# A fused retention and latent-attention trunk: the last four modulation vectors moved from the retention stage to the latent stage, and rows turned to columns by DMA

## The chip, the cores and the metric

The kernel runs on one core of a Trainium2 chip. Its time is device microseconds (us) of one execution. The engines are TensorE (PE in the profile, PEld its weight loads), VectorE (DVE), ScalarE (ACT), GpSimd (POOL) and SyncE (SP), which here does little but issue DMAs.

## The reference, cut to what matters

Everything is float32, with 256 tokens of width 1024 and two layers. Layer 0 mixes by retention, layer 1 by latent attention (MLA) over a key and value side made from the stream after layer 0. Both have a mixture of 16 experts, two chosen for each token.

```python
c_act = silu(c)                                   # one row of 1024
for layer in range(2):
    mod = c_act @ w_mod[layer] + b_mod[layer]     # 1024 x 6144
    sh1, sc1, g1, sh2, sc2, g2 = split(mod, 6)
    if layer == 0:
        xn = rms_norm(h, norm_mix[0]) * (1 + sc1) + sh1
        mix = retention_mixer(xn, ...)            # w_in 1024 x 6144, w_out 2048 x 1024
    else:
        sh_kv, sc_kv = split(c_act @ w_mod_kv + b_mod_kv, 2)
        hn = rms_norm(h, norm_kv) * (1 + sc_kv) + sh_kv
        k_nope, k_rope, v = mla_shared_kv(hn, ...)
        xn = rms_norm(h, norm_mix[1]) * (1 + sc1) + sh1
        mix = mla_attention(xn, ..., k_nope, k_rope, v)
    h = h + g1 * mix
    xn = rms_norm(h, norm_ffn[layer]) * (1 + sc2) + sh2
    h = h + g2 * grouped_moe(xn, ...)             # 16 experts of 3 x 2.1 MB
return rms_norm(h, final_norm)
```

So there are 14 modulation vectors: six of each layer and two for the key and value side. Four of them are gates (g1, g2 of both layers), the others are shifts and scales. Layer 1's g1 is first used when the attention's output product is done, and its sh2, sc2 and g2 in its experts.

## The kernel before, in words

**Streaming.** Nearly all bytes are weights, each read once. SP loads them in a fixed order into a ring of six slots of 2.1 MB (L139). Item i waits until item i-6 is used up (`released`, L406 to L414); every item is loaded as two halves. SP works strictly in order, so an item whose slot is not free holds back all behind it. `STREAM` (L101 to L117) is the order for the retention stage: blocks of the input matrix (`win`), halves of modulation vectors (`mod`) and blocks of the output matrix (`wout`). A vector's 4.2 MB are two `mod` items m = 2v and 2v+1 of vector v in `MODV` (L78): v = 2 and 5 are layer 0's gates, 10 and 13 layer 1's gates; 11 and 12 are layer 1's sh2 and sc2.

**A vector.** DVE multiplies an item into a tile `part` with four instructions of 128x1024 (`mod_main`, L1463), each waiting for the one before. PE then sums over the partitions: for a gate with a matrix of ones, two products of 128x512 into bank 5, each added to the gate's bias by DVE (`gate_sum` L594, `gate_store` L1486; bank 5 is one buffer, so the second product waits for the first store); for a shift or scale with a one-hot block, into one row of bank 4 (L611 to L616). All eight rows stay in that bank. After the last, ACT copies the bank to SBUF and PE turns the rows to columns with 24 small products, once in the order that modulates activations (L766) and once in the order that the router wants (L769). DVE adds the biases and makes the scales (L1569 to L1584) and folds layer 0's scale into the router's weights (`router_prep`, L1586).

**Retention.** Twelve rounds, one for each `win` block, of 13.7 us of matmuls and small work (L675 to L730). `MODS_PER_ROUND` (L103) says which modulation items a round handles: one in round 2, three in round 3 and two in each after it. The four that remain (`LAST_MODS`, 24 to 27) are handled among the eight blocks of the output product (`wout`, L745 to L773).

**Experts.** For each of 8 pairs of experts, a round of 25.9 us on PE per 64 tokens of the busier expert: gather, gate, up and down products. Layer 0 has 8 rounds, layer 1 has 9 (one pair needs two). The next pair's gate, up and down matrices (12.6 MB) are loaded as this pair's are used up (`reload`, L458). Ahead of the first pair SP issues its two gate and two up matrices, waits for the attention's (or the retention's) last heads, issues its down matrices into space outside the ring (L441 to L450), then the second pair's gate matrices (L451).

**Latent stage.** Its six items (L125) take the six slots as layer 0's last experts free them. PE makes the latents (L999, L1007, L1015), DVE and ACT normalise them, PE turns and expands them (L1022 to L1063), then come eight heads and the output product (L1122). `router_prep(1)` stands ahead of the latents on DVE (L1752), and `fixed_logits(1)` behind L999 on PE.

## Time and profile before

| what | value |
|---|---|
| time, median of 3 runs | 935.76 us (935.08 to 938.44) |
| the profiled execution's own time | 935.13 us |
| its span, first to last instruction | 933.4 us |
| PE busy | 860.8 us, 92% |
| DVE, ACT, POOL busy | 323.8, 171.1, 156.8 us |
| DMA | 317.12 MB, mean 340 GB/s |
| chain that ended last | PE 72%, DMA 17%, DVE 5% |

The profile follows one execution. Its part 2 cuts the span into 40 slices of 23.3 us and shows how busy each engine was, the TensorE clock that was granted, and what the DMA moved. The chain is followed back from the last instruction, at each step to what released it. Times of rows count from the span's start.

### The profile page before, as it was taken

How to read it: one execution, taken by the hardware profiler on the slowest of the kernel's cores; microseconds unless marked ns; L12 is line 12 of the kernel's file. 1: busy time of each engine (PE TensorE's matmuls, PEld its weight loads, DVE VectorE, ACT ScalarE, POOL GpSimd, SP SyncE). 2: the span in 40 equal slices, each digit the busy share in tenths (PEclk: the TensorE clock that was granted, in tenths of full speed). 3: DMA queues.
4: the chain of work that ended last, by engine and by line, in shares of the span. 5: the costliest groups of instructions: out<-in, count | busy, mean ns of one | idle time of the engine just before them, and what ended most of it. 6: DMA issues, size and time to landing. Idle time of an engine off the chain costs nothing.

```text
span 933.4 us, 12095 instructions
## 1 busy us (share of the span) xinstructions
PE 860.8 (92%) x4387; PEld 479.3 (51%) x4388; DVE 323.8 (35%) x592; ACT 171.1 (18%) x339; POOL 156.8 (17%) x272
## 2 busy tenths in 40 slices
PE   6996899999999799999899879899899999999985
PEld 3785344444445554555354428684455554555442
DVE  2748568669723411111111123350411111111103
ACT  2100011121100312221201111251322212211111
POOL 0022100000001721222200121400632221111011
PEclk9998899999999899999989898999899999999988
DMA  9999999899847989999999995525469999399995
GB/s 324 387 357 372 369 377 381 326 378 379 317 180 323 403 328 421 415 422 422 423 422 421 388 358 213 206 90 202 159 249 424 416 396 422 137 390 423 422 379 170
DMA packets 68645, 317.12 MB, mean 340 GB/s; under 512 B 8935, under 2 KB 9066, under 8 KB 43262
## 3 DMA queue, kind: packets, MB, share of 16 engines
q1 hardware_dynamic: 61274, 304.42, 81.6%
q0 software_dynamic: 4976, 8.40, 3.6%
q10 hardware_dynamic: 2356, 3.76, 1.2%
q8 instruction: 26, 0.43, 0.2%
q14 instruction: 13, 0.11, 0.0%
HBM read 311.31 MB, written 15.20 MB: 350 GB/s over the span
## 4 chain that ended last, share of the span: by engine, by line
PE 72%; DMA 17%; DVE 5%; issue 2%; ACT 1%; SPq 1%; POOL 0%; ACTq 0%; DVEq 0%; POOLq 0%
PE bank L701 12%; PE bank L887 12%; DMA ring<-in_moe_w_up 8%; PE bank L905 8%; PE bank L874 8%; PE bank L739 6%; DMA h<-outs 6%; PE bank L849 5%; PE bank L642 3%; PE bank L1122 3%; DMA outs<-arena,row_id 2%; DVE part L1478 2%; PE bank L1077 1%; PE bank L897 1%; DMA ring<-in_w_mod 1%
## 5 line engine op out<-in xcount | busy, mean ns | idle before, releaser
L887 PE MATMUL bank<-ring,arena 128*64 128x256 f32 x1088 | 132.6, 399 | 18.7 <-DMA ring<-in_moe_w_up 18.7
L887 PEld LDWEIGHTS bank<-ring,arena 128*64 128x64 f32 x1088 | 83.8, 144 | 68.1 <-issue 39.1
L1722 DVE TENSOR_TENSOR arena<-bank,arena 128x256 f32<-128x256 f32 x34 | 20.9, 616 | 277.0 <-PE bank L887 277.0
L1478 DVE SCALAR_TENSOR_TENSOR part<-ring,cpad,part 128x1024 f32<-128x1024 f32 x84 | 109.0, 1297 | 21.2 <-DMA ring<-in_w_mod 16.4
L701 PE MATMUL bank<-ring,xnT 128*128 128x512 f32 x256 | 112.1, 596 | 0.0
L905 PE MATMUL bank<-ring,arena 128*64 128x512 f32 x480 | 109.3, 596 | 2.5 <-issue 2.5
L874 PE MATMUL bank<-ring,arena 128*64 128x512 f32 x480 | 106.3, 595 | 0.0
L701 PEld LDWEIGHTS bank<-ring,xnT 128*128 128x128 f32 x256 | 48.6, 192 | 61.7 <-issue 61.7
L849 PEld LDWEIGHTS bank<-arena,y 128*128 128x128 f32 x544 | 66.7, 204 | 17.5 <-issue 17.5
L849 PE MATMUL bank<-arena,y 128*128 128x128 f32 x544 | 69.8, 290 | 3.4 <-issue 3.4
L874 PEld LDWEIGHTS bank<-ring,arena 128*64 128x64 f32 x480 | 33.1, 137 | 60.2 <-issue 60.0
L905 PEld LDWEIGHTS bank<-ring,arena 128*64 128x64 f32 x480 | 33.3, 137 | 58.9 <-issue 56.7
L1274 ACT ACTIVATE arena<-bank,modc,scale 128x128 f32<-128x128 f32 x68 | 25.6, 456 | 184.4 <-PE bank L849 184.4
L1876 POOL DMA_INDIRECT outs<-arena,row_id x17 | 17.9, 1056 | 216.1 <-DVE arena L1732 135.6
L1732 DVE SCALAR_TENSOR_TENSOR arena<-bank,info,gate 128x512 f32<-128x512 f32 x34 | 25.5, 751 | 73.2 <-PE bank L905 73.2
L1852 POOL TENSOR_TENSOR h<-h,acc 128x512 f32<-128x512 f32 x6 | 7.5, 1265 | 255.3 <-DVE acc L1604 255.2
L1871 POOL TENSOR_SCALAR arena<-slot_id,place_two 128x64 f32<-128x64 f32 x108 | 45.8, 445 | 5.5 <-POOL slot_id L1886 3.0
L642 PE MATMUL bank<-xnT,ring 128*128 128x256 f32 x192 | 41.9, 379 | 0.0
L642 PEld LDWEIGHTS bank<-xnT,ring 128*128 128x128 f32 x192 | 36.4, 190 | 5.3 <-DVE xnT L1432 0.5
L1713 DVE TENSOR_SCALAR arena<-bank,scale,modc 128x128 f32<-128x128 f32 x68 | 23.2, 405 | 27.6 <-PE bank L849 27.6
L739 PE MATMUL bank<-ring,arena 128*128 128x512 f32 x64 | 29.5, 619 | 0.0
L1122 PE MATMUL bank<-ring,arena 128*128 128x512 f32 x64 | 27.7, 593 | 0.5 <-issue 0.5
(304 smaller groups left out, 863.2 us busy)
## 6 DMA issues: line engine op xcount, KB each, us to landing
ring<-in_moe_w_up SPq DMA_DIRECT2D x64, 1024.0 KB, 14.0
ring<-in_moe_w_gate SPq DMA_DIRECT2D x56, 1024.0 KB, 14.7
ring<-in_moe_w_down SPq DMA_DIRECT2D x56, 1024.0 KB, 16.3
ring<-in_w_mod SPq DMA_DIRECT2D x48, 1024.0 KB, 12.1
ring<-in_ret_w_in SPq DMA_DIRECT2D x24, 1024.0 KB, 11.5
ring<-in_w_mod_kv SPq DMA_DIRECT2D x8, 1024.0 KB, 13.2
ring<-in_ret_w_out SPq DMA_DIRECT2D x8, 1024.0 KB, 9.4
arena<-in_moe_w_down SPq DMA_DIRECT2D x2, 2048.0 KB, 15.3
```

What stands on the lines that cost most here:

```text
L642: ins = pe.matmul(o[:, f * SEQ:(f + 1) * SEQ], w[:, k, c:c + P], xnT[:, k, :], start=(f == 0 and k == 0), stop=(f == 1 and k == KT - 1))
L701: ins = pe.matmul(pair[tt][:], xnT[:, k, tok(tt)], w[:, k, :], start=(k == 0), stop=(k == KT - 1))
L739: ins = pe.matmul(bank[2 * tt + n][:], yT(4 * i + kk)[:, tok(tt)], w[:, kk, n * 512:(n + 1) * 512], start=(i == 0 and kk == 0), stop=(i == ...
L849: ins = pe.matmul(bank[4 + k // 4][:, (k % 4) * P:(k % 4 + 1) * P], y[:, tt, k * P:(k + 1) * P], chosen_slots[:, tt, :], start=(tt == 0), ...
L874: ins = pe.matmul(bank[0][e * 64:(e + 1) * 64, :], xgT[:, k, e * 64:(e + 1) * 64], w(e, k), start=(k == 0), stop=(k == KT - 1))
L887: ins = pe.matmul(bank[1 + f][e * 64:(e + 1) * 64, 0:256], xgT[:, k, e * 64:(e + 1) * 64], w(2 + e, k)[:, f * 256:(f + 1) * 256], start=(k ...
L905: ins = pe.matmul(bank[6 + n2][e * 64:(e + 1) * 64, :], hidT[:, k, e * 64:(e + 1) * 64], w(4 + e, k)[:, n2 * 512:(n2 + 1) * 512], start=(k ...
L1122: ins = pe.matmul(mla_bank[(5, 6, 7, 0)[2 * tt + n]][:], oT[:, 4 * i + kk, tok(tt)], w[:, kk, n * 512:(n + 1) * 512], start=(i == 0 and kk ...
L1274: ins = A(xgT[:, k, :], bank[5][:, tok(j)], ACT.Identity, bias=modc[:, MOD_COL[l] + 24 + k:MOD_COL[l] + 25 + k], scale=scale[:, 1 + 2 * l, ...
L1478: ins = dve.scalar_tensor_tensor(o, w[:, k, :], c, o, ALU.mult, ALU.add)
L1732: dve.scalar_tensor_tensor(yg[:, s], bank[6 + n2][:], info[:, 1:2], gate[:, 2 * l + 1, s], ALU.mult, ALU.mult).then_inc(S["yg_ready"], 1)
L1871: ins = pool.tensor_scalar(dst[:, tt, e * SLOTS:(e + 1) * SLOTS], slots, places[:, tt, e:e + 1], None, ALU.is_equal)
```

## The change

The last eight modulation items (m = 20 to 27: layer 1's g1, sh2, sc2 and g2) leave the retention stage's stream. Each round of retention now has two items at most, and the output product none. The eight items stand in the latent stage's list (`MLA_ITEMS`) instead: 20 and 21 take the slots that the output matrix `wo` had, 22 to 25 those of the latent matrices once these are used up, then come the two `wo` items, then 26 and 27. The first four matrices of layer 1's experts now follow item 24, item 25, `wo0` and `wo1`.

On DVE the items are multiplied at five places: 20 and 21 behind the modulation of activations, 22 ahead of the latents' norm, 23 in two parts around the query's rotation, 24 to 27 behind the last head. On PE the gate's two sums stand ahead of the turned latents, sh2's row ahead of the scores and sc2's among the blocks of the output product. The last gate's sums stand in the routing of layer 1, in the place of two products that had no other use, and its stores behind the routing's last instruction on DVE; PE waits for them before the rounds.

The eight rows go in four pairs. ACT copies a pair, and issues two small DMAs that lay the rows out as columns in `turned` (`copy_rows`); PE turns only the two pairs that the router wants (`turn_ffn`, 8 products of two columns each).

```diff
-MODS_PER_ROUND = (0, 0, 1, 3, 2, 2, 2, 2, 2, 2, 2, 2)
+MODS_PER_ROUND = (0, 0, 0, 1, 2, 2, 2, 2, 2, 2, 2, 1)
...
-STREAM += [("wout", i) for i in range(3)] + [("mod", m) for m in LAST_MODS[:3]] + [("wout", 3)]
-STREAM += [("mod", m) for m in LAST_MODS[3:]]
+STREAM += [("wout", i) for i in range(4)]
...
-MLA_ITEMS = ["kva", "qa", "kvb", "qb", "wo0", "wo1"]
+MLA_ITEMS = [("kva", 0), ("qa", 0), ("kvb", 0), ("qb", 0)] + [("mod", m) for m in range(LATE_MOD, LATE_MOD + 6)]
+MLA_ITEMS += [("wo0", 0), ("wo1", 0)] + [("mod", m) for m in range(LATE_MOD + 6, N_MOD)]
...
+            def row_sum(v, b):
+
+                pe.wait_ge(mod_sum, 2 * v + 2)
+                at = C_ROW + P - 1 - ROW_OF[v][1]
+                for g in range(2):
+                    ins = pe.matmul(b[32 * g:32 * g + 32, :], cst[:, at:at + 32], part[:, v % 2, g * 512:(g + 1) * 512],
+                                    start=(ROW_OF[v][1] == 0), stop=(ROW_OF[v][1] == 1))
+                ins.then_inc(mod_folded, 1)
...
+            def turn_ffn(g, b):
+
+                pe.wait_ge(rows_copied, g + 1)
+                for k in range(KT):
+                    ins = pe.matmul(b[:, 2 * k:2 * k + 2], row_tile[g][:, (k % 4) * P:(k % 4 + 1) * P],
+                                    ident[0:64, 32 * (k // 4):32 * (k // 4) + 2], start=True, stop=True)
+                ins.then_inc(vecs_turned, 1)
...
+                if r == 9:
+                    pe.wait_ge(mod_stored, MOD_STORED[(5, 1)])
+                    turn_ffn(0, bank[5])
...
-            mod_gather(LAST_MODS[0])
             wout(2, 0)
-            mod_gather(LAST_MODS[1])
             wout(2, 1).then_inc(wo_used, 1)
-            mod_gather(LAST_MODS[2])
...
-                keep_warm(2, 7)
+                if l == 0:
+                    keep_warm(2, 7)
+                else:
+                    pe.wait_ge(mod_sum, N_MOD)
+                    gate_sum(13, 0, bank[1])
+                    gate_sum(13, 1, bank[2])
...
                 pe.wait_ge(table_ready, l + 1)
+                if l:
+                    pe.wait_ge(mod_stored, MOD_STORED[(13, 1)])
...
+            pe.wait_ge(mod_sum, LATE_MOD + 2)
+            pe.wait_ge(kr_mult, 2)
+            gate_sum(10, 0, mla_bank[5])
+            gate_sum(10, 1, mla_bank[3])
             pe.wait_ge(lat_norm, 2)
...
+            pe.wait_ge(qr_mult, 4)
+            row_sum(11, mla_bank[6])
...
+                        if (i, tt, n) == (0, 1, 0):
+                            row_sum(12, mla_bank[6])
+                        if (i, tt, n) == (1, 0, 0):
+                            turn_ffn(3, mla_bank[2])
+                        if (i, tt, n) == (1, 1, 0):
+                            fixed_logits(1, mla_bank[3])
...
+            def copy_rows(g, b):
+
+                act.wait_ge(mod_folded, FOLDED_ALL[ROW_PAIRS[g][1]])
...
+                A(row_tile[g], b[0:64, :], ACT.Copy).then_inc(rows_copied, 1)
...
+                for r in range(2):
+                    act.dma_start(turned[:, g, r, :], row_tile[g][r:64:32, :].rearrange("g (p k) -> g p k", k=KT)).then_inc(vecs_in, 16)
...
+            def vectors(g, bias):
+
+                c = (MOD_COL[0] + 3 * KT, MOD_COL[2], MOD_COL[1], MOD_COL[1] + 3 * KT)[g]
+                dve.wait_ge(vecs_in, 32 * (g + 1))
...
             normed(2)
-            router_prep(1)
             modulate(2, hnT, 4, MOD_COL[2])
             modulate(2, xnT, 2, MOD_COL[1])
+            mod_main(20)
+            mod_main(21)
...
+            mod_main(22)
 
             dve.wait_ge(lat_sq, 4)
...
-            mixed(1, (1, 2, 3, 4))
+            for m in range(24, N_MOD):
+                mod_main(m)
+            vectors(3, cols[:, :, 10:12])
+            scales(3, MOD_COL[1] + 32, gcol[:, :, 3])
+            ffn_vectors(1, mla_bank[2])
+            router_prep(1)
+            mixed(1, (1, 3, 4, 0))
```

On PE, from the matmuls of round 3 into round 4 of retention, before:

```order
L694 MATMUL bank<-xnT,ring 128x256 x32
L598 MATMUL bank<-part,cst 128x512 x2
L614 MATMUL bank<-part,cst 32x512 x2
L701 MATMUL bank<-ring,xnT 128x512 x16
L712 MATMUL bank<-arena 128x256 x2
L715 MATMUL bank<-arena 128x128 x2
```

The same place now, where L715 is round 3's matmuls, L722 those of rounds 4 and 5, L604 a gate's sum and L611 a row's:

```order
L715 MATMUL bank<-xnT,ring 128x256 x32
L722 MATMUL bank<-ring,xnT 128x512 x16
L733 MATMUL bank<-arena 128x256 x2
L736 MATMUL bank<-arena 128x128 x2
L604 MATMUL bank<-part,cst 128x512 x2
L722 MATMUL bank<-ring,xnT 128x512 x16
L611 MATMUL bank<-part,cst 32x512 x2
```

The gate's two sums moved from ahead of round 4's matmuls to behind them, and the row's sum into round 5.

On DVE, in the latent stage from the modulation of activations to the copies of the expanded latents, before:

```order
L1390 TENSOR_SCALAR xnT<-bank,scale,modc 128x256 x4
L1759 TENSOR_TENSOR acc<-bank,arena 128x512 x2
L1763 TENSOR_SCALAR stat<-stat 128x2
L1764 TENSOR_SCALAR stat<-stat 128x2
L1766 RECIPROCAL stat<-stat 128x4
L1768 TENSOR_SCALAR arena<-bank,stat 128x128 x2
L1770 TENSOR_SCALAR xnT<-bank,stat 128x256 x2
L1773 TENSOR_SCALAR arena<-bank,lat_gain 128x256 x2
L1776 COPY arena<-bank 128x512 x2
```

The same place now; L1514 and L1516 are the products of items 20, 21 and 22, L1801 is the key's rotation and L1532 the gate's stores:

```order
L1514 TENSOR_SCALAR part<-ring,cpad 128x1024
L1516 SCALAR_TENSOR_TENSOR part<-ring,cpad,part 128x1024 x7
L1801 TENSOR_TENSOR acc<-bank,arena 128x512 x2
L1514 TENSOR_SCALAR part<-ring,cpad 128x1024
L1516 SCALAR_TENSOR_TENSOR part<-ring,cpad,part 128x1024 x3
L1806 TENSOR_SCALAR stat<-stat 128x2
L1807 TENSOR_SCALAR stat<-stat 128x2
L1809 RECIPROCAL stat<-stat 128x4
L1811 TENSOR_SCALAR arena<-bank,stat 128x128 x2
L1813 TENSOR_SCALAR xnT<-bank,stat 128x256 x2
L1816 TENSOR_SCALAR arena<-bank,lat_gain 128x256 x2
L1532 TENSOR_TENSOR gate<-bank,gate 128x512 x2
```

Item 22's four products now stand between the key's rotation and the latents' norm.

On SP, from the latent matrices to layer 1's first experts, before:

```order
L396 DMA ring<-in_mla_w_q_b 128x1536 x2
L396 DMA ring<-in_mla_w_o 128x2x1024 x4
L396 DMA ring<-in_moe_w_gate 128x2048 x4
L396 DMA ring<-in_moe_w_up 128x2048 x4
L448 DMA arena<-in_moe_w_down 128x2x2048
L450 DMA arena<-in_moe_w_down 128x2048
```

The same place now:

```order
L398 DMA ring<-in_mla_w_q_b 128x1536 x2
L398 DMA ring<-in_w_mod 128x2x1024 x12
L398 DMA ring<-in_mla_w_o 128x2x1024 x4
L398 DMA ring<-in_w_mod 128x2x1024 x4
L398 DMA ring<-in_moe_w_gate 128x2048 x4
L398 DMA ring<-in_moe_w_up 128x2048 x4
L450 DMA arena<-in_moe_w_down 128x2x2048
```

Sixteen halves of modulation items now stand ahead of the experts' first matrices, twelve of them ahead of the output matrix too.

## Rows read from the trace of the kernel before

**Rows 1.** Of the page, part 2: GB/s that the DMA moved, 40 equal slices.

```profile
GB/s 324 387 357 372 369 377 381 326 378 379 317 180 323 403 328 421 415 422 422 423 422 421 388 358 213 206 90 202 159 249 424 416 396 422 137 390 423 422 379 170
```

**Rows 2.** Busy time by stretch: PE, PEld, DVE, ACT, POOL, then PEclk, DMA share, GB/s.

```profile
100.00:135.00 35.00, 34.72 (x87) 15.55 (x86) 20.70 (x20) 5.89 (x6) 0.00 (x0) 0.98 0.97 368
...
346.00:372.00 26.00, 26.00 (x170) 13.41 (x168) 4.52 (x9) 5.26 (x10) 5.44 (x13) 1.00 1.01 422
...
580.00:584.00 4.00, 4.00 (x21) 3.51 (x20) 0.00 (x0) 0.00 (x0) 0.00 (x0) 1.00 0.98 401
...
616.00:620.00 4.00, 4.00 (x30) 3.68 (x29) 2.06 (x11) 2.04 (x9) 0.00 (x0) 1.00 0.00 0
...
672.00:676.00 4.00, 2.32 (x10) 1.93 (x10) 1.54 (x9) 1.28 (x1) 2.96 (x8) 0.50 0.02 6
...
684.00:688.00 4.00, 4.00 (x24) 1.58 (x22) 0.00 (x0) 0.59 (x1) 2.37 (x5) 1.00 0.73 246
```

**Rows 3.** The timeline of PE, retention: start, us, instructions, [idle before <-releaser].

```profile
96.35 2.08 PE L598 MATMUL bank<-part,cst 128*128 128x512 f32 x2 [10.53 <-DVE gate L1491]
...
100.21 14.69 PE L701 MATMUL bank<-ring,xnT 128*128 128x512 f32 x32
...
151.37 1.05 PE L614 MATMUL bank<-part,cst 128*32 128x512 f32 x4
```

**Rows 4.** The same, output product of layer 0 and what follows.

```profile
240.48 13.90 PE L739 MATMUL bank<-ring,y 128*128 128x512 f32 x32
...
254.65 7.03 PE L739 MATMUL bank<-ring,y 128*128 128x512 f32 x16
...
293.58 1.95 PE L769 MATMUL bank<-cst,arena 64*128 64x8 f32 x16
...
304.98 0.29 PE L778 MATMUL bank<-shifted,cst 128*128 128x16 f32 x2
...
318.13 6.36 PE L849 MATMUL bank<-arena,y 128*128 128x128 f32 x32 [1.70 <-issue]
```

**Rows 5.** The timeline of DVE: a gate store, and the products of two items.

```profile
98.47 0.69 DVE L1491 TENSOR_TENSOR gate<-bank,gate 128x512 f32<-128x512 f32 x1 [2.17 <-PE bank L598]
...
222.50 0.74 DVE L1476 TENSOR_SCALAR part<-ring,cpad 128x1024 f32<-128x1024 f32 x1
...
223.28 3.93 DVE L1478 SCALAR_TENSOR_TENSOR part<-ring,cpad,part 128x1024 f32<-128x1024 f32 x3
...
227.43 5.25 DVE L1478 SCALAR_TENSOR_TENSOR part<-ring,cpad,part 128x1024 f32<-128x1024 f32 x4 [0.21 <-DVE part L1478]
```

**Rows 6.** The timelines of SP, DVE, PE and DVE in the latent stage.

```profile
578.13 7.71 SPq L396 DMA_DIRECT2D ring<-in_moe_w_gate  x4
...
585.92 0.17 DVE L1763 TENSOR_SCALAR stat<-stat 128x2 f32<-128x2 f32 x1 [6.49 <-ACT xnT L1315]
...
587.30 0.45 PE L1022 MATMUL bank<-cst,arena 128*128 128x128 f32 x2 [2.30 <-DVE arena L1768]
...
598.70 1.29 DVE L1786 TENSOR_TENSOR acc<-bank,arena 128x512 f32<-128x512 f32 x2 [2.34 <-PE bank L1051]
```

**Rows 7.** The timeline of PE, two waits of the expert rounds.

```profile
529.60 8.11 PE L887 MATMUL bank<-ring,arena 128*64 128x256 f32 x48 [4.05 <-DMA ring<-in_moe_w_up]
...
792.90 5.40 PE L887 MATMUL bank<-ring,arena 128*64 128x256 f32 x48 [1.78 <-DMA ring<-in_moe_w_up]
```

**Rows 8.** The timelines of PE and, last, DVE: output product and routing, layer 1.

```profile
634.10 27.71 PE L1122 MATMUL bank<-ring,arena 128*128 128x512 f32 x64 [0.52 <-issue]
...
661.64 1.47 PE L792 MATMUL bank<-cst,h 128*128 128x128 f32 x12
...
674.10 5.90 PE L849 MATMUL bank<-arena,y 128*128 128x128 f32 x32 [1.68 <-issue]
...
673.43 0.25 DVE L1695 TENSOR_SCALAR back_id<-in_last 128x4 int32<-128x4 f32 x1
```

**Rows 9.** DMA issues: size, median us from issue to landing.

```profile
br<-in_router_b ACTq DMA_DIRECT2D x1, 8.0 KB, 7.8
```

165 lines of the change are left out of this document (83 added, 82 removed).

## The prediction, made before the changed kernel had run

> **What bounds the kernel now.** I read part 2 of the page first: the DMA moves some 420 GB/s in most expert slices, 350 to 390 in retention, and falls to 90 to 250 in slices 25 to 30 [rows 1]. 16.8 MB are moved into that hole. So the question is what their transfer costs where it is now. The table by stretch answers: from 100 to 135 us PE is busy 34.72 of 35 us with the DMA's share at 0.97 [rows 2]. Retention stands near both limits, but PE is the one that sets its pace, and loads taken from it give back only what PE loses to them. The timeline of PE shows two such places. Ahead of round 4 PE waits 10.53 us for a gate's store by DVE [rows 3]. The output product takes from 240.48 to 304.98 us [rows 4], 64.5 us for eight blocks of 6.87 (the step from the row at 254.65 to the next block). In the expert rounds the order is reversed: 26 us of PE work against a DMA at 422 GB/s and a share of 1.01 [rows 2], with PE waiting 4.05 and 1.78 us for up matrices [rows 7].
>
> **Part 1, retention.** Before, round 3's matmuls end at 96.35 - 10.53 - 0.86 = 84.96 us (0.86 is one product of 128x512, an eighth of the 6.87), and round 4 starts at 100.21 [rows 3]. Now nothing stands between them: one item is left in rounds 2 and 3, and round 4's block is released earlier in the stream. That is -15.25. In the rounds, by durations of 0.86 for a gate's sum, 0.98 for a row's (1.05 less what the next product overlaps), and 1.95 for 16 small passes [rows 3, 4]: both sums of one gate now stand together in rounds 4 and 7, and the second waits for the first's store, about 1.2 us (store 0.69 [rows 5], and two handovers). Round 4 gains a sum and this wait and loses 0.9 us of half-clock start, +0.7; round 7 +1.8; round 9 gains the small turn, +1.7; rounds 6 and 11 lose a sum each, -1.8; rounds 5 and 10 +0.2. Together +2.6. DMA per round is as before, three items or 6.3 MB, 16.6 us at 380 GB/s against rounds of 17 to 19, and a block is asked for over a round ahead, so I cost it at nothing; without this cover a round would grow by under 1 us.
>
> **Part 2, output product of layer 0.** Now 8 x 6.87 + 0.87 for turning the last head = 55.84 instead of 64.50: -8.66. The columns by DMA are issued about 20 us ahead of their use. Behind it the routing took 318.13 - 304.98 = 13.15 us; layer 1, whose blocks follow one another evenly as they now do here, took 674.10 - 661.64 = 12.46 [rows 4, 8], with 0.15 to add: -0.5. Layer 0's experts start 15.25 - 2.6 + 8.7 + 0.5 = 21.8 us earlier. Their own length I leave unchanged: though their first matrices are asked for long before, the reach ahead is limited by space, and the next loads wait for the first round's gate product as before. What could be gained (0 to 3 us, if a backlog of the first matrices had delayed them) I take at 0.
>
> **Part 3, latent stage.** Items 20 and 21 are 4.7 and 5.4 us of DVE (0.74 + 3.93, and 5.25 and a handover [rows 5]) in an idle stretch of 11 us; nothing. Item 22 is the one that hurts. Its slot comes free at 578.13, where SP issued a gate matrix [rows 6]; 2.1 MB at 401 GB/s [rows 2] and some 1.5 us around it land it at 585.0 to 585.5. DVE waits for it, works to about 590.1, and only then does the latents' norm, which started at 585.92 [rows 6]: +4.2 (bounds 3.6 and 6). Queued behind it are the norm, the turned latents on PE, and all after these. PE, with 1.7 us of gate sums in between, now idles some 4.7 us where it idled 2.30 [rows 6]. In the expert rounds a wait of 4.05 us is followed by 48 products that take 8.11 us instead of 5.40, one of 1.78 is not [rows 7]; the granted clock's half level of 1.2 GHz shows as such a stretch. So I add 2.6 us (bounds 0 and 2.7). The gate's stores (1.3 us) then hide behind the slower products; without the slow clock they cost 0.8. Item 23's first half is 2.65 us in an idle 2.34 [rows 6], its second in a like one: 0.1 at most. sh2's row costs 0.98 of which the wait for copies hides 0.8: +0.2. Part 3 is +7.0.
>
> **Part 4, output product of layer 1.** sc2's row 0.98, the small turn 1.95, the fixed logits 0.15: +3.05 on the 27.6 us between the first two of [rows 8]. DVE has items 24 to 27 (20.6 us) in the time in which it waited for the fifth block, and ends about with it. The routing's two sums replace two products of the same length. The stores do not hide: DVE ends its routing at 673.43 + 0.25 [rows 8], two stores make 675.05, and PE, which was through at 672.42 (its start less the 1.68 idle), reads its loop bounds only after them: +2.65, and 0.3 for the half clock at its start. Part 4 is +6.0.
>
> **Part 5, layer 1's experts.** Before, 13.6 MB of their matrices had landed when the output product ended; now 6.3, since the second up matrix waits for `wo1` and SP is in order. 10.5 MB are asked for at the product's end: 25 us at 420 GB/s. The next loads are asked for 15.1 + 9.9 = 25.0 us after it (routing with its stores, then gather and half the gate product), and before they moved from about 10.8 us after the start ([rows 2], the stretch from 684). The gap in which the DMA was idle, 0.02 at 672 [rows 2], just takes them. I add 0.3, bounds 0 and 5.
>
> The Trainium skill ("DMA: Bandwidth & Descriptors", Where 436 GB/s comes from) puts HBM to SBUF at some 358 GB/s for a core. By that the 10.5 MB would take 29.3 us, and the lag and the total would grow by about 4 us. The trace disagrees: 422 GB/s over whole rounds [rows 2], from HBM.
>
> **Sum.** -21.8 + 7.0 + 6.0 + 0.3 = -8.5 against the profiled execution's 935.13, so 926.6. That run lies 0.6 below the median of the runs, 935.76; I predict 927.2.
>
> **Rivals.** (a) The clock stays up in the latent stage: the gate sums break the idle stretch. For it: each part is shorter than 4.05 us or near it; against: the second part alone is about 4.7. Time 927.2 - 1.8 = 925.4.
> (b) The last columns come late. They are issued at about 653 us of the old scale and wanted at 661, with some 4 us to spare behind. An 8 KB load of short runs took 7.8 us [rows 9]. At 16 us DVE's chain and with it the routing start 5 us later: 932.
> The Trainium skill (same page, Specifications) says that transfers under 512 B fall below line rate, and these runs are 32 B. The trace has no SBUF to SBUF copy of this kind; 8 KB are so little that the rate matters less than the queue.
> (c) The other side: the experts' first matrices are not absorbed. Each us by which the 10.5 MB outlast the next loads' call is a us of waiting at pair 4, as the DMA has no slack up to there (the wait of 1.78 us at 792.90 [rows 7] is the proof). If nothing of the 7.3 MB that are missing were absorbed, the cost is 17.5 us, 927.2 + 17.5 = 944.7, slower than before. It decides at 0.9 us of slack, from 25.0 to 25.9. Against it: the idle gap in [rows 2].
> (d) Retention is bound by its DMA: then 16.8 MB at 380 GB/s are 44 us, and the time is 935.8 - 44 + 13.3 = 905. Against it: PE's 34.72 of 35.
> (e) The change does not free round 4: block 4 or items 5 and 6, asked for only when earlier blocks are used up, land late and half the hole stays: 935.
>
> **How the numbers follow.** My forecast with its own spread (923 to 931) 0.50, (a) 0.19, (b) 0.12, (c) 0.06, (d) 0.03, (e) 0.10. The range reaches from 922 into (b) and stops at 933. A measurement tells about 0.5% here, 4.7 us, so faster means under 931.1: nearly all of the forecast and of (a), and (d), less some of the spread: 0.76. Same takes (b), (e) and the spread's upper end: 0.17. Slower is (c) and a sum of mishaps: 0.07.
>
> **What would show it.** Right: no idle stretch of PE between rounds 3 and 4; the output product of layer 0 at about 56 us; layer 0's experts at 296 us; a wait of DVE for item 22 that ends near 563 of the new scale (585 - 21.8) and an idle stretch of PE of 4 to 5 us with a clock of 0.5 behind it; the output product of layer 1 at 30.6 us; 15 us from its end to the experts; a wait at pair 4 of about 2 us. Wrong: experts of layer 0 later than 300 us, an item 22 that lands before the norm wants it, or a wait at pair 4 of over 4 us.

## The result, and the profile after

The changed kernel took 928.45 us (median of 18 runs, 924.82 to 932.75), the one before 935.02 us (18 runs, 930.72 to 939.1). The ratio is 0.993 with a 95% interval of 0.9912 to 0.9949: some 6.6 us, or 0.7%, faster. A second comparison with the same kernel (e10 below) gave 0.9913 (0.9896 to 0.9931), 8 us. The forecast was 927.2 us, 8.5 us faster, range 922 to 933. The profiled execution of the changed kernel took 930.08 us with a span of 928.3.

The view that carries most of the comparison is the timeline of PE. Where does a stage start in it, and how far has that moved from the same row of before? First retention, the output product of layer 0 and the first round of experts, with the columns as in [rows 3].

```profile
77.72 7.07 PE L715 MATMUL bank<-xnT,ring 128*128 128x256 f32 x32
84.63 13.90 PE L722 MATMUL bank<-ring,xnT 128*128 128x512 f32 x32
...
99.67 1.02 PE L604 MATMUL bank<-part,cst 128*128 128x512 f32 x2
101.48 0.70 PE L604 MATMUL bank<-part,cst 128*128 128x512 f32 x1 [0.78 <-DVE gate L1532]
...
227.48 13.90 PE L763 MATMUL bank<-ring,y 128*128 128x512 f32 x32
...
283.30 0.29 PE L787 MATMUL bank<-shifted,cst 128*128 128x16 f32 x2
...
296.48 3.78 PE L865 MATMUL bank<-arena,y 128*128 128x128 f32 x17 [0.26 <-issue]
```

Round 4 starts at 84.63 us where it started at 100.21 [rows 3]; the wait of 10.53 us and the sums behind it are gone. The output product starts at 227.48 instead of 240.48, and takes 55.82 us to the row at 283.30 instead of 64.50 [rows 4]. The experts start at 296.48 instead of 318.13: 21.65 us won.

From here on the gain shrinks. The same view in layer 0's last round, the latent stage, layer 1's output product and its experts:

```profile
522.87 6.49 PE L921 MATMUL bank<-ring,arena 128*64 128x512 f32 x16 [4.50 <-issue]
...
540.61 3.81 PE L558 MATMUL bank<-cst,y 128*128 128x128 f32 x16 [5.04 <-DVE y L1419]
545.67 5.44 PE L1015 MATMUL bank<-ring,arena 128*128 128x128 f32 x32 [1.26 <-ACT arena L1203]
...
573.57 0.69 PE L1039 MATMUL bank<-cst,arena 128*128 128x128 f32 x2 [6.92 <-DVE arena L1811]
...
575.26 5.87 PE L1053 MATMUL bank<-arena,ring 128*128 128x256 f32 x16
...
623.14 2.38 PE L1143 MATMUL bank<-ring,arena 128*128 128x512 f32 x5 [0.52 <-issue]
...
669.47 6.64 PE L865 MATMUL bank<-arena,y 128*128 128x128 f32 x32 [4.85 <-issue]
...
788.39 5.40 PE L903 MATMUL bank<-ring,arena 128*64 128x256 f32 x48 [1.17 <-DMA ring<-in_moe_w_up]
...
897.25 7.07 PE L903 MATMUL bank<-ring,arena 128*64 128x256 f32 x48 [4.58 <-DMA ring<-in_moe_w_up]
```

Layer 1's output product starts at 623.14 instead of 634.10, the experts at 669.47 instead of 674.10 [rows 8]. The wait at pair 4 stands at 1.17 us instead of 1.78 [rows 7]. So 21.65 us ahead became 10.96, then 4.63, and 5.1 at the end.

The row at 573.57 names its cause: 6.92 us of idle, released by DVE's normed latents. On DVE one sees what they waited for:

```profile
558.32 1.28 DVE L1801 TENSOR_TENSOR acc<-bank,arena 128x512 f32<-128x512 f32 x2
567.31 0.75 DVE L1514 TENSOR_SCALAR part<-ring,cpad 128x1024 f32<-128x1024 f32 x1 [7.71 <-issue]
568.09 3.92 DVE L1516 SCALAR_TENSOR_TENSOR part<-ring,cpad,part 128x1024 f32<-128x1024 f32 x3
572.18 0.17 DVE L1806 TENSOR_SCALAR stat<-stat 128x2 f32<-128x2 f32 x1 [0.16 <-DVE part L1516]
```

Item 22 lands at 567.3, is multiplied for 4.7 us, and only then comes the norm. (The row names no releaser, but SP asked for the item's second half at 558.46, and it landed at 567.22.) The norm started at 585.92 before [rows 6], which on the new scale (19.58 us earlier, by the latents' first product) is 566.34.

One view more, from the tail of layer 0's experts: POOL's issues and, last, DVE's additions into h.

```profile
505.00 1.36 POOL L2004 DMA_DIRECT2D h<-outs  x1 [0.34 <-POOL row_id L2001]
520.59 1.22 POOL L2004 DMA_DIRECT2D h<-outs  x1 [14.23 <-DMA h<-outs]
```

```profile
534.38 2.48 DVE L1748 TENSOR_TENSOR h<-bank,h 128x512 f32<-128x512 f32 x4 [4.23 <-DMA h<-outs]
```

The reader is to see that PE's slow products at 522.87 cost nothing. They end at 529.3, but DVE adds into h only when the second return of expert rows has landed, at 534.4.

Of the page, part 2, the GB/s by slices, to be laid beside [rows 1]:

```profile
GB/s 323 387 357 376 373 330 376 348 316 383 146 320 139 307 424 402 420 422 422 423 423 415 331 207 182 187 361 267 309 397 423 416 396 423 141 390 423 423 379 179
```

The hole in slices 25 to 30 is half filled: slices 26 to 29 show 187, 361, 267 and 309 where 206, 90, 202 and 159 stood.

### The profile page after: what moved, and what is told of

It reads as the page before. It is cut to its first block, busy times and chain, and to the rows that moved or that the text cites. A ratio compares the mean times of both kernels' runs of the same rounds, so it can differ in the third digit from the quotient of the medians.

```text
span 928.3 us, 12079 instructions
## 1 busy us (share of the span) xinstructions
PE 859.1 (93%) x4367; PEld 480.4 (52%) x4368; DVE 325.8 (35%) x592; ACT 172.5 (19%) x342; POOL 162.2 (17%) x272
## 4 chain that ended last, share of the span: by engine, by line
PE 76%; DMA 16%; DVE 3%; issue 2%; ACT 1%; SPq 1%; ACTq 0%; DVEq 0%; POOL 0%; POOLq 0%
PE bank L903 13%; PE bank L722 12%; DMA ring<-in_moe_w_up 11%; PE bank L921 8%; PE bank L890 8%; PE bank L763 6%; PE bank L865 5%; PE bank L663 4%; DMA h<-outs 3%; PE bank L1143 3%; PE bank L715 1%; PE bank L1096 1%; PE bank L913 1%; DMA outs<-arena,row_id 1%; PE bank L549 1%
## 5 line engine op out<-in xcount | busy, mean ns | idle before, releaser
L903 PE MATMUL bank<-ring,arena 128*64 128x256 f32 x1088 | 130.1, 394 | 16.7 <-DMA ring<-in_moe_w_up 16.7
L921 PE MATMUL bank<-ring,arena 128*64 128x512 f32 x480 | 112.2, 609 | 5.8 <-issue 5.8
L1516 DVE SCALAR_TENSOR_TENSOR part<-ring,cpad,part 128x1024 f32<-128x1024 f32 x84 | 111.2, 1324 | 3.2 <-DVE part L1516 0.7
L722 PE MATMUL bank<-ring,xnT 128*128 128x512 f32 x256 | 111.2, 593 | 0.0
L890 PE MATMUL bank<-ring,arena 128*64 128x512 f32 x480 | 106.3, 596 | 0.0
L722 PEld LDWEIGHTS bank<-ring,xnT 128*128 128x128 f32 x256 | 48.5, 190 | 59.3 <-issue 59.2
L1143 PE MATMUL bank<-ring,arena 128*128 128x512 f32 x64 | 28.5, 598 | 0.5 <-issue 0.5
L763 PE MATMUL bank<-ring,y 128*128 128x512 f32 x64 | 28.0, 592 | 0.0
```

The costliest lines, as they stand in the source:

```text
L722: ins = pe.matmul(pair[tt][:], xnT[:, k, tok(tt)], w[:, k, :], start=(k == 0), stop=(k == KT - 1))
L763: ins = pe.matmul(bank[2 * tt + n][:], yT(4 * i + kk)[:, tok(tt)], w[:, kk, n * 512:(n + 1) * 512], start=(i == 0 and kk == 0), stop=(i == ...
L890: ins = pe.matmul(bank[0][e * 64:(e + 1) * 64, :], xgT[:, k, e * 64:(e + 1) * 64], w(e, k), start=(k == 0), stop=(k == KT - 1))
L903: ins = pe.matmul(bank[1 + f][e * 64:(e + 1) * 64, 0:256], xgT[:, k, e * 64:(e + 1) * 64], w(2 + e, k)[:, f * 256:(f + 1) * 256], start=(k ...
L921: ins = pe.matmul(bank[6 + n2][e * 64:(e + 1) * 64, :], hidT[:, k, e * 64:(e + 1) * 64], w(4 + e, k)[:, n2 * 512:(n2 + 1) * 512], start=(k ...
L1143: ins = pe.matmul(mla_bank[(5, 7, 0, 4)[2 * tt + n]][:], oT[:, 4 * i + kk, tok(tt)], w[:, kk, n * 512:(n + 1) * 512], start=(i == 0 and kk ...
```

## The experiments

All are edits of the changed kernel. Each was timed in four to six runs, one of them profiled, beside the kernel before, so their ratios to it can be compared with the 0.993 and 0.9913 of the changed kernel; two of them can be told apart only when they lie about 0.003 apart.

| kernel | median, us | ratio to before | 95% interval |
|---|---|---|---|
| e1 item 22 late | 921.8 | 0.9864 | 0.9845 to 0.9882 |
| e2 warm gap | 926.68 | 0.9912 | 0.9893 to 0.9931 |
| e3 no store wait | 926.75 | 0.9924 | 0.9902 to 0.9946 |
| e4 items early | 942.91 | 1.0082 | 1.006 to 1.0105 |
| e5 order before layer 1 | 928.27 | 0.9931 | 0.9913 to 0.9949 |
| e6 loads behind the returns | 927.44 | 0.9925 | 0.9908 to 0.9943 |
| e7 = e1 + e3 | 921.54 | 0.9861 | 0.9845 to 0.9877 |
| e8 = e1 + e3 + e5 + e6 | 918.6 | 0.9818 | 0.9805 to 0.983 |
| e9 = e1 + e6 | 922.36 | 0.9858 | 0.9838 to 0.9878 |
| e10 the changed kernel again | 927.0 | 0.9913 | 0.9896 to 0.9931 |
| e11 = e1 + e3 + e5 | 922.41 | 0.9863 | 0.9835 to 0.989 |
| e12 = e3 + e5 | 925.49 | 0.99 | 0.987 to 0.993 |

From each trace the length of the stages was read on PE's timeline, from the first row of one stage to the first of the next. "Experts 0" runs from their first row to the turning of y behind them (296.48 and 540.61 in the rows above), "latents" from the row at 545.67 to layer 1's output product at 623.14, "end to experts 1" from the end of that product, and "experts 1" from their first row to the end of the span.

| trace | experts 0 | latents | end to experts 1 | experts 1 |
|---|---|---|---|---|
| before | 242.04 | 68.85 | 12.29 | 259.30 |
| after | 244.13 | 77.47 | 15.15 | 258.83 |
| e10 | 246.18 | 73.31 | 15.15 | 258.20 |
| e2 | 245.11 | 73.81 | 15.16 | 258.56 |
| e3 | 244.65 | 74.44 | 12.27 | 260.85 |
| e4 | 245.83 | 73.17 | 15.16 | 257.57 |
| e5 | 245.48 | 73.26 | 15.21 | 257.68 |
| e6 | 243.27 | 75.73 | 15.16 | 257.29 |
| e12 | 242.91 | 77.63 | 12.28 | 258.56 |
| e1 | 247.18 | 69.17 | 14.79 | 259.62 |
| e7 | 243.27 | 69.17 | 12.28 | 258.92 |
| e9 | 241.68 | 71.11 | 14.79 | 257.82 |
| e11 | 244.50 | 70.72 | 12.38 | 258.55 |
| e8 | 243.20 | 71.32 | 12.32 | 258.23 |

**e1, item 22 later.**

```
DVE   mod_main(22)               # was here, ahead of the norm: gone
      dve.wait_ge(lat_sq, 4)
      ...
-     mod_main(23, (0, 1))       ...   mod_main(23, (2, 3))
+     mod_main(22, (0, 1))       ...   mod_main(22, (2, 3))
      ...                        # in heads 2 to 5, behind head_max(hd + 2)
+     mod_main(23, (hd - 2,))
PE  - row_sum(11, mla_bank[6])   # ahead of scores(0)
    + row_sum(11, mla_bank[6])   # ahead of the output product
```

> Edit: item 22 of the modulation no longer stands before the latents' norm on DVE but in two halves where item 23 stood; item 23 is spread over four heads of the attention, and the row sum of items 22 and 23 on PE moves from before the first scores to before the output product. Theory (the wait for item 22's landing and the slow clock behind it are the cost of the latent stage): DVE's norm starts at 566.4 instead of 572.18, PE's idle stretch before the turned latents falls from 6.92 us to about 1, the sixteen products behind it take 3.6 us instead of 5.87; together -5.8 - 2.3 = -8.1 us, some 920.5 against 928.5. Rival 1 (the clock falls in any case, by the shorter waits there): -5.8, 922.7. Rival 2 (DVE is the bound in the attention's heads: 5.2 us of item 23 lie in gaps of 1.23 us and push each head): half is given back, 924.5. Rival 3 (the layer's experts are held by their matrices, whose requests depend on other things): the experts start 8 us earlier and wait as much longer at pair 4, 928.

Measured: 0.9864, 4.6 to 6.2 us less than the changed kernel; 921.8 lies between the theory and rival 1. The timeline of PE in its trace, where its stretch starts 5.24 us later than in the trace of after:

```profile
568.38 1.88 PE L604 MATMUL bank<-part,cst 128*128 128x512 f32 x4
570.83 0.44 PE L1039 MATMUL bank<-cst,arena 128*128 128x128 f32 x2 [0.58 <-DVE arena L1808]
571.62 0.66 PE L1044 MATMUL bank<-cst,xnT 128*128 128x128 f32 x4 [0.35 <-DVE xnT L1810]
572.11 1.89 PE L1053 MATMUL bank<-arena,ring 128*128 128x256 f32 x8
574.44 1.99 PE L1053 MATMUL bank<-arena,ring 128*128 128x256 f32 x8 [0.43 <-DVE gate L1531]
```

The idle stretch is 0.58 us instead of 6.92, and the sixteen products take 3.9 us, so rival 1's slow clock isn't there. The latents take 69.17 us, 8.3 less than in the trace of after and 4.1 less than in e10's. (The profiled run of e1 is with 927.46 us the slowest of its six; its retention and layer 0's experts, which the edit doesn't touch, took 2.2 and 3.0 us longer than in after.) Rival 2 took its part, but a small one: from the first scores to the output product 27.78 us instead of 26.04, of which 1.0 is the row sum that moved in, and 0.7 the heads. The mechanism is shown. For its size the traces have to be compared by how fast the latents' first 32 products ran, which the edit doesn't touch either. Where they took 3.81 us the latents last 69.17 us with item 22 late (e1, e7) and 73.2 to 74.4 without (e3, e4, e5, e10). Where they took 5.3 to 5.95 us it is 70.7 to 71.3 (e8, e9, e11) against 75.7 to 77.6 (after, e6, e12). That is 4.4 and 5.9 us on the average, and the totals say 4.6 to 6.2.

**e2, PE kept busy in the gap.**

```
       gate_sum(10, 1, mla_bank[3])
+      keep_warm(7, 3)
       pe.wait_ge(lat_norm, 2)
```

> Edit: seven products of 128x512 that nobody reads are put on PE between the gate's sums and the wait for the normed latents, in the idle stretch of 6.92 us. Nothing else moves. Theory (the slow stretch behind the wait is a cost of its own, 2.25 us, and comes from the idle stretch): the sixteen products behind it take 3.6 us instead of 5.87 and the time falls by 2 us, to 926.4. Rival 1 (the clock would fall anyway, or another unit sets the pace behind it, DVE's gate stores and copies): no change, 928.5. Rival 2 (the added products end late): slower by up to 1 us.

Measured: 0.9912, as e10's 0.9913. The sixteen products did become fast (rows of PE):

```profile
565.76 6.17 PE L549 MATMUL bank<-cst 128*128 128x512 f32 x14
572.81 0.44 PE L1040 MATMUL bank<-cst,arena 128*128 128x128 f32 x2 [0.87 <-DVE arena L1812]
573.59 0.66 PE L1045 MATMUL bank<-cst,xnT 128*128 128x128 f32 x4 [0.34 <-DVE xnT L1814]
574.09 1.89 PE L1054 MATMUL bank<-arena,ring 128*128 128x256 f32 x8
576.41 1.99 PE L1054 MATMUL bank<-arena,ring 128*128 128x256 f32 x8 [0.43 <-DVE gate L1533]
```

From the turned latents to the first scores it took 21.54 us, against 23.53 in after, 22.52 in e10 and 22.13 in e3. The sixteen products with their wait for DVE's stores (0.43) go from 574.09 to 578.25, 4.16 us, against 5.71 in after (575.26 to 580.97, where the next group starts). The table by stretch shows the granted clock over the same eight microseconds, counted from about the turned latents, in after, in e10 and here (the first number behind the brackets, 1.00 being 2.4 GHz and 0.50 the half level of 1.2 GHz):

```profile
573.00:581.00 8.00, 7.34 (x23) 5.84 (x24) 4.06 (x9) 1.67 (x3) 5.18 (x6) 0.57 0.00 1
```

```profile
572.00:580.00 8.00, 7.51 (x25) 5.69 (x26) 4.58 (x10) 1.80 (x4) 5.34 (x7) 0.71 0.02 6
```

```profile
572.00:580.00 8.00, 6.41 (x27) 4.44 (x28) 4.86 (x11) 2.27 (x4) 5.39 (x7) 1.00 0.01 2
```

So the slow clock is there in after and e10 and gone here, and it costs 0.6 to 2 us, not 2.25 each time. In the total it can't be told from nothing.

**e3, no wait for the gate's stores.**

```
       pe.wait_ge(table_ready, l + 1)
-      if l:
-          pe.wait_ge(mod_stored, MOD_STORED[(13, 1)])
```

> Edit: PE no longer waits for the two stores of layer 1's second gate before it starts the experts; the order is kept by the wait of each round for DVE's gathered columns, which stand behind the stores on DVE. Theory (the stores stand on the path, as the prediction's Part 4 said): the experts start 2.65 us earlier and without the 0.7 us of slow clock, -3 us, 925.4. Rival 1 (the routing's other waits end as late): -1 or less, 927.5. Rival 2 (what is won at the start is lost at pair 4, where the DMA is the bound): the wait there grows from 1.17 to about 4 us and the time stays at 928.5.

Measured: 0.9924, between the two ratios of the changed kernel. The trace shows both halves of rival 2, the second smaller than it said. PE's timeline:

```profile
663.55 5.70 PE L863 MATMUL bank<-arena,y 128*128 128x128 f32 x32 [1.23 <-issue]
...
782.81 7.09 PE L901 MATMUL bank<-ring,arena 128*64 128x256 f32 x48 [2.44 <-DMA ring<-in_moe_w_up]
```

The end of the product to the experts fell from 15.15 to 12.27 us, the 2.9 that were forecast for the stores. The wait at pair 4 is 2.44 us (1.17 in after, 0.48 in e10), the 48 products behind it took 7.09 us instead of 5.40, and the experts took 260.85 us, 2.0 and 2.7 us more than in after and e10.

**e4, items back in the early rounds.**

```
-MODS_PER_ROUND = (0, 0, 0, 1, 2, 2, 2, 2, 2, 2, 2, 1)
+MODS_PER_ROUND = (0, 0, 1, 3, 2, 2, 2, 2, 2, 2, 0, 0)
-    if r in (7, 9):  copy_rows(0 if r == 7 else 1, bank[4])
+    if r in (5, 7):  copy_rows(0 if r == 5 else 1, bank[4])
```

> Edit: the retention's sixteen items are spread as before the change (1 and 3 of them in rounds 2 and 3, none in the last two rounds); with them the first two copies of rows move two rounds ahead. The other parts of the change stay. Theory (PE's wait ahead of round 4 was the cost, and it was removed by moving these items): about 10.5 us of idle and 4 us of sums come back before round 4, some 3 us of sums leave the later rounds, +11 to +13 us, about 940.5. Rival 1 (the four items fewer are what helped, the retention is bound by its DMA): no change, 928.5. Rival 2 (half each): 934.

Measured: 1.0082, slower than before, and 14 to 16 us slower than the changed kernel. PE's timeline ahead of round 4:

```profile
84.21 1.02 PE L604 MATMUL bank<-part,cst 128*128 128x512 f32 x2
96.33 2.08 PE L604 MATMUL bank<-part,cst 128*128 128x512 f32 x2 [11.10 <-DVE gate L1532]
98.33 1.92 PE L611 MATMUL bank<-part,cst 128*32 128x512 f32 x4
100.18 2.11 PE L722 MATMUL bank<-ring,xnT 128*128 128x512 f32 x4
```

The hole is back, round 4 starts 15.55 us later, and 3.0 come back in the later rounds: 12.53 at the start of the output product. The total moved by 1 to 3 us more than the theory's 13, while the profiled run, the fastest of its six with 938.86 us, lies 9 to 12 above the changed kernel's. This is the largest single part of the change, and a DMA bound on retention as its source (rival 1 here, rival (d) of the prediction) is excluded.

**e5, the order of loads ahead of layer 1.**

```
-  for j in range(4):                       # all four first matrices
+  for j in range(3 if l else 4):
       released(base - RING + j);  load(base + j, matrix(l, 0, j))
   ...                                      # down matrices, next pair's gates
+  if l:
+      released(base - RING + 3);  load(base + 3, matrix(l, 0, 3))
   sp.wait_ge(h_ready, 4 * l + 4)
```

> Edit: only the order of SP's loads ahead of layer 1's experts. The second up matrix, whose slot comes free with the last block of the output product, is asked for after the two down matrices and the two gate matrices of the next pair instead of before them; 6.3 MB can so move while the output product runs, where the DMA stood at 131 GB/s. Theory (layer 1's experts are bound by the DMA, so that what is asked for late is paid for in their waits): the waits of 1.17 us at pair 4 goes and the one of 4.58 us at the last pair shrinks by some 3, with the slow products behind it (1.7 us): from the experts' start to the end 256 instead of 258.8 us, 926. Rival 1 (the prefetch is early enough, the prediction's Part 5, and the rounds are bound by PE): no change, 928.5. Rival 2 (the up matrix now comes too late for the first round): it lands some 21 us after 655, at 676 to 680, PE wants it at 682; if late, slower by 1 to 5 us.

Measured: 0.9931. The loads did move. The table by stretch for the second half of layer 1's output product, first of after, then of e5 (the last number is GB/s):

```profile
640.00:655.00 15.00, 15.00 (x55) 7.97 (x54) 5.35 (x14) 3.72 (x8) 6.05 (x4) 1.00 0.32 131
```

```profile
640.00:655.00 15.00, 14.70 (x77) 8.49 (x80) 6.10 (x15) 5.64 (x13) 7.61 (x4) 1.00 1.01 427
```

The wait at pair 4 did not go: it is 0.66 us, less than after's 1.17 and more than e10's 0.48. The one before the last pair stayed (4.80 us, after 4.58). The length of the experts, 257.68, lies in the spread of the others. So 1.2 us of wait at most were there to win, and rival 1, which is the prediction's Part 5, holds.

**e6, four loads held behind the returns of expert rows.**

```
-  for j, (kind, n) in enumerate(MLA_ITEMS):
+  for j in [0, 1, 4, 5, 2, 3] + list(range(6, len(MLA_ITEMS))):
+      kind, n = MLA_ITEMS[j]
+      if j == 4:
+          freed(2, total)
+          sp.wait_ge(back_in, 32)
```

> Edit: SP asks for four loads behind layer 0's experts (items 20 and 21, then the key-value and query up projections) only when both returns of expert rows into h by POOL's DMA have landed. Theory (the end of layer 0's experts is set by those two returns, and the second runs beside SP's loads: 13.8 us there against 9.4 in layer 1, where nothing else moves): DVE's last additions start some 4 us earlier, at 530 to 531 instead of 534.4, and what stands behind moves with them; items 20 and 21 land by about 545; -4 us, 924.5. Rival 1 (the second return is not slowed by these loads, but by the down matrices or by itself): no change, 928.5. Rival 2 (the projections land late: asked for at 531 behind 4.2 MB, they land at about 548, wanted at 575; items 20 and 21 late, and with them item 22): the gain is given back in the latent stage, 928.

Measured: 0.9925, no change that can be told. The step itself did what was expected. POOL's second issue stands at 523.00 us and DVE adds at 533.52, 10.5 us behind it instead of 13.8 (11.6 in e8 and 12.4 in e9, which have the edit too; 13.0 to 15.0 in the ten traces of changed kernels without it). From the last round to the turning of y it took 44.24 us, where the ten have 46.4 to 49.0, 48.1 on the average. The gain of 4 us did not arrive at the end. It was not rival 2: the loads came in time (the latents are not longer here than in after or e12). The latents' first products ran slow instead (5.53 us for 32) as in after, and the latents took 75.73 us where e10 has 73.31. The rounds ahead of the tail took 199.0 us in this trace, 2.2 more than the ten on the average, for no reason that the trace names.

**e7, e8 and e9, combinations.**

> Edit: those of e1_item22_late and e3_no_store_wait together. Alone they gave 921.8 and 926.75 against 928.45. Theory (the two act at different places, but layer 1's experts are bound by the DMA: in e3's trace their start moved 2.9 us and their length grew by 2 us): 921.8 - 1 = 920.8. Rival (they add up by the trace of the start alone): 921.8 - 2.9 = 918.9.

Measured: 0.9861, no less than e1 alone. So the stores brought nothing that can be told; the theory's 1 us is under what can be measured. The trace does not bear out its reason: PE's wait at pair 4 is 1.42 us, but the experts start 2.5 us sooner than in e1 (12.28 against 14.79) and take 258.92 us, no longer than e1's 259.62. The growth of e3's trace did not come again.

> Edit: the four of e1, e3, e5 and e6 together. Theory: 928.5 - 6.7 (item 22) - 4 (returns) - 2.9 (stores, now covered by the earlier loads) - 2.5 (order) = 912.4. Rival 1 (the order of loads and the returns bring nothing): as e7, 920.8. Rival 2 (the DMA in the latent stage is the bound once the waits are gone, since item 22's and the later slots all come free in turn): 917.

Measured: 0.9818, 918.6 us: 16.7 us faster than before and the best version here, but 6 us short of the theory and between the two rivals.

> Edit: those of e1_item22_late and e6_back_alone together, SP's order ahead of layer 1 and PE's wait for the stores as in the changed kernel. Alone they gave 0.986 and 0.9925 of the time before, the changed kernel 0.993, all four together 0.9818. Theory (only these two touch the path; the order of loads and the stores are worth nothing, since layer 1's experts end with the same 258 us after their start or give it back in waits): as all four, 0.982 of the time before, 918.6. Rival 1 (it takes the stores and the order as well, covered only together): 0.985, 921.5. In the trace: from the last round of layer 0's experts to the next turn of y 45 us instead of 47.5 to 48.7, and from the latents' first product to layer 1's output product 69 us.

Measured: 0.9858, rival 1. The tail was 45.86 us as expected, but the latents 71.11 and not 69, with 5.64 us for their first products instead of the 3.81 of e1.

**e10, the changed kernel again.**

> The changed kernel once more, with no edit, beside the same runs of the kernel before: a second profiled execution of it. The first had three slow stretches of PE that traces of other kernels with the same code there don't have (16 products in 6.49 us behind a wait in layer 0's last round, the latents' first 32 in 5.44, the sixteen behind the norm in 5.87). Theory (they and the time at which item 22 lands differ from one execution to the next): from the latents' first product to layer 1's output product some 73 to 75 us here instead of 77.5, with 68.85 before, and a median of 0.993 of the time before. Rival (they belong to this kernel): 77 to 78 us again.

Measured: 0.9913, and 73.31 us for the latents: the theory. PE's timeline at the places where after was slow:

```profile
523.50 3.65 PE L921 MATMUL bank<-ring,arena 128*64 128x512 f32 x16 [2.82 <-issue]
...
542.57 3.65 PE L558 MATMUL bank<-cst,y 128*128 128x128 f32 x16 [9.22 <-DVE y L1419]
547.66 3.81 PE L1015 MATMUL bank<-ring,arena 128*128 128x128 f32 x32 [1.43 <-DVE xnT L1427]
...
572.40 0.69 PE L1039 MATMUL bank<-cst,arena 128*128 128x128 f32 x2 [5.40 <-DVE arena L1811]
...
574.09 4.88 PE L1053 MATMUL bank<-arena,ring 128*128 128x256 f32 x16
```

With no edit at all, three groups took 3.65, 3.81 and 4.88 us instead of 6.49, 5.44 and 5.87. The wait for item 22 was shorter too, for two reasons of about equal size. The products ahead of it, whose end frees its slot, were fast, so SP asked for it 10.75 us behind the latents' first product instead of 12.38. And its second half landed 7.2 us after it was asked for instead of 8.8; the other traces have 7.3 to 7.4 us (e1, e4, e5, e7) or 8.3 to 8.9 (the rest), for no reason that they show.

**e11 and e12, what the best version owes to which part.**

> Edit: the four of e8_all_four without that of e6 (SP's loads are not held behind the returns of expert rows). Theory (holding the loads is worth nothing: what it takes from the tail of layer 0's experts comes back as slow products in the latent stage, 5.64 and 5.95 us for the first 32 in two traces with it, 3.81 in four without): 0.982 of the time before, as e8. Rival (it is part of the best version): 0.986, as e7 and e9, 922.

> Edit: those of e3 (no wait for the gate's stores) and e5 (order of SP's loads ahead of layer 1) together, item 22 where the changed kernel has it. Theory (they cover each other: the earlier start was paid back in the DMA's waits, 260.85 us from the experts' start to the end in e3's trace, and the earlier loads had nothing to cover in e5, 257.68): together the start moves 2.5 to 2.9 us and the length stays at 258, 3 us less than the changed kernel, 0.9895 of the time before, 925.2. Rival (as small as each alone): 0.992, 927.5.

Measured: e11 0.9863, the rival's number; e12 0.99, the theory's (0.9895). The lengths of e12 fit the theory: 12.28 us to the experts with 258.56 us of experts, where e3 had 260.85, and waits at pair 4 of 0.37 to 0.55 us in the three traces with both edits (e8, e11, e12) against 2.44 and 1.42 with the stores alone (e3, e7). But e7 took 258.92 us without the earlier loads, so the cover they give is at most this microsecond or two. e12's interval reaches to 0.993, though, so the total alone would not prove it. And e11 against e7 shows no such gain. That e8 is better than e11, and so what holding the loads adds, rests on intervals that just miss each other (0.9805 to 0.983, and 0.9835 to 0.989), while e9 against e1 shows nothing. This stays open.

## Why the prediction was right, step by step

The table sets each step beside what two traces of the same kernel show, after and e10, as the difference to the trace of before in us. Routing 0 is from the end of the output product to the experts; the 5 us between the turning of y and the latents' first product are equal in all.

| step | forecast | after | e10 |
|---|---|---|---|
| Part 1, retention | -12.65 | -13.00 | -13.04 |
| Part 2, output product and routing 0 | -9.15 | -8.65 | -8.70 |
| layer 0's experts | 0 | +2.09 | +4.14 |
| Part 3, latents | +7.0 | +8.62 | +4.46 |
| Part 4, product of layer 1 | +3.05 | +3.47 | +3.47 |
| Part 4, its end to the experts | +2.95 | +2.86 | +2.86 |
| Part 5, layer 1's experts | +0.3 | -0.47 | -1.10 |
| sum | -8.5 | -5.1 | -7.9 |

**Right, to half a microsecond: Parts 1, 2 and 4.** The hole before round 4 went as a whole (e4 brings it back), the second sum of a gate waits 0.78 us for a store (1.2 forecast), the output product takes 55.82 us (55.84 forecast). The 0.5 us that Part 2 gave to the routing did not come: 13.18 us from 283.30 to 296.48, before 13.15. In layer 1 the product grew by what the sums and turns in it cost, and the stores stood on the path with 2.9 us (e3).

**Right in mechanism, and in size only on the average: Part 3.** DVE waits for item 22 and the norm comes late. Against the trace of before it is 5.8 us in after and 2.7 in e10 (571.01 us, where 568.33 would keep before's distance to the latents' first product), between which the forecast of 4.2 lies. But the first 32 products took 5.72 us in before and 3.81 in e10, which has nothing to do with the change and takes 1.9 us off e10's figures. Against traces whose first products were as fast, e1 for e10 (the norm 18.54 us behind the first product, and 23.35) and e11 for after (20.06 and 26.51), the norm is 4.8 and 6.4 us late. So the forecast, with its bounds of 3.6 and 6, was low by 0.6 and 2.2, and Part 3 as a whole is 6.4 us in e10 and 8.9 in after instead of the 4.46 and 8.62 of the table. (Item 22's landing was foreseen near 563 us and came at 567.2 and 566.1; the stage itself began 2.2 us later than foreseen in after and 4.2 in e10.) The slow clock behind the wait is there as well: against e2, where it was kept up, it cost 2.0 us in after and 1.0 in e10, forecast 2.6. e1 shows that all of it hung on where item 22 stood.

**Part 5** lies 0.8 and 1.4 us under its forecast of +0.3, within the spread of the experts' length. The wait at pair 4, foreseen at about 2 us, was 1.17 and 0.48, so the loads were absorbed as forecast.

**The step that failed: "Their own length I leave unchanged ... I take at 0".** Layer 0's experts take 244.9 us on the average of the ten traces without e6's edit, 2.9 more than in the one trace of before. I had looked for a gain there and not for a loss. The end of this stage is set by two returns of expert rows, not by PE, and the prediction read no row of this tail. From the last round on, the ten take 48.1 us and before 46.03; the rounds ahead of it differ by -0.3 to +2.5 us. e6 shows that SP's loads slow the second return (10.5 to 12.4 us in three traces, 13.0 to 15.0 in the ten). But before has such loads too, and its return took 13.3 us, within the spread of the ten, so the difference isn't shown to come from them. What the traces do show is that this stage comes in two kinds, told apart by the wait for the last up matrix. Here it is in e12 and in after:

```profile
508.15 8.13 PE L904 MATMUL bank<-ring,arena 128*64 128x256 f32 x48 [4.08 <-DMA ring<-in_moe_w_up]
```

```profile
506.77 5.40 PE L903 MATMUL bank<-ring,arena 128*64 128x256 f32 x48 [2.35 <-DMA ring<-in_moe_w_up]
```

In e7 and e12 it is 4.0 and 4.1 us, as in before (4.05 [rows 7]), and the stage takes 243.27 and 242.91 us, 1.2 and 0.9 more than before. In the other eight it is 2.3 to 2.5 us, and the stage takes 244.1 to 247.2. So one trace of before can't tell how much of the 2.9 us belongs to the change and how much to that execution. The cause stays open.

**What was luck.** The forecast stood 1.3 us under the measured median, and 0.2 over that of e10. It added 8.5 us of gain, counted on one execution, to a median of three runs that the 18 later ones put 0.7 lower. The gain itself was 6.6 and 8 us. In e10 the unforeseen 4.14 us of layer 0's experts were nearly made good by Part 3, which came 2.5 us under its forecast (1.9 of it by the fast first products), and by Part 5 (1.4).

**Rivals.** (a), that the clock stays up, is wrong: with item 22 ahead of the norm the granted clock is 0.50 in the two us behind the turned latents' start in all seven traces (after, e3 to e6, e10, e12), and only how long it stays there differs, from 0.6 to 2.1 us of cost. (b), late columns: the last two were asked for at 635.3 and 636.4 us and used at 640.63, without a wait; wrong. (c), layer 1's matrices: the wait at pair 4 fell; wrong for this change, but e3 and e7 show the bound standing close behind it, as the prediction put it ("It decides at 0.9 us of slack"): the experts start 2.9 us earlier, and the wait at pair 4 grows to 2.44 us in e3 and 1.42 in e7. (d) and (e) are excluded by e4 and by the row at 84.63.

The Trainium skill's figure on HBM ("DMA: Bandwidth & Descriptors", Where 436 GB/s comes from) had been set against [rows 2] with the trace as the judge. The stretch of e5 above, 427 GB/s, again disagrees with some 358.

## What to carry to other kernels

A load that is asked for late must not stand in an in-order engine's program ahead of small work that others wait for: move its consumer back to where its data has long been there, and see that what it releases isn't needed sooner. Read each stage's end back to what released it (here a DMA return, not PE's products) before taking its length as fixed. And a stage of one profiled execution carries 2 to 4 us that belong to that execution, the one of the kernel before no less than the others; several traces with the same code in a stage are worth more than one read to a hundredth.

## What the runs showed of the hardware

**The tail and the latent stage trade with each other.** In the traces where the turning of y was preceded by an idle stretch of 4.1 to 5.3 us (before, after, e6, e8, e9, e11, e12), the latents' 32 first products took 5.3 to 5.95 us. Where it was 6.3 to 9.2 us long (e1 to e5, e7, e10) they took 3.81. The longer wait was followed by the faster products. The table by stretch gives the granted clock (PEclk, the first number behind the brackets) as 0.50 in after and 0.67 in e10 over the turning of y, and then 0.74 and 1.00 over the six us behind it:

```profile
540.00:546.00 6.00, 4.13 (x17) 3.49 (x18) 4.89 (x11) 2.61 (x8) 0.68 (x1) 0.50 0.87 344
546.00:552.00 6.00, 6.00 (x37) 5.90 (x37) 5.89 (x6) 1.98 (x7) 5.57 (x4) 0.74 0.06 23
```

```profile
542.00:548.00 6.00, 4.00 (x19) 3.50 (x20) 4.89 (x11) 2.62 (x7) 0.64 (x1) 0.67 0.57 226
548.00:554.00 6.00, 6.00 (x45) 5.69 (x44) 5.89 (x6) 1.96 (x7) 5.57 (x4) 1.00 0.01 3
```

This takes back 1.5 to 2.1 us where the tail is 2.2 to 3.8 us shorter (e6, e8, e9). It is one reason why e6 and e9 show no gain at the end; that it is the whole reason isn't shown. What decides when the half level of 1.2 GHz begins after work stops isn't settled by these rows.

**DVE and POOL slow each other.** The second half of item 23 takes 2.6 us for two products elsewhere. Beside POOL's two it took 3.48, and POOL's took 2.24 and 2.25, where the same two took 1.27 and 1.26 in the trace of before. Rows of DVE, POOL, POOL:

```profile
590.50 3.48 DVE L1516 SCALAR_TENSOR_TENSOR part<-ring,cpad,part 128x1024 f32<-128x1024 f32 x2
...
590.66 2.24 POOL L2045 TENSOR_TENSOR arena<-acc 128x512 f32<-128x512 f32 x1 [7.34 <-DVE acc L1832]
...
592.87 2.25 POOL L2046 TENSOR_TENSOR arena<-acc 128x512 f32<-128x512 f32 x1
```

The Trainium skill ("SBUF — State Buffer", Who interferes with whom) says that an operation of VectorE with both inputs in SBUF contends with one of GpSimd that reads SBUF, and that the pair of ports they share is locked by one of them at a time. The trace agrees that they hold each other up: all three rows are longer. It does not show a strict turn: alone the four would take 5.1 us in sequence, and together they took 4.6 from the first start to the last end, though spans on POOL are rough. It cost nothing here, as the queries' copies behind it were in time. Item 20 and POOL's copies of the rotated weights collide in the same way: 5.04 us for three products instead of 3.93.
